# State-space stage of a decoder trunk: six output pieces in another order, column units between the inputs, a lag of 12 instead of 16, three early gated weights

## What is computed

```
u = h @ in_w                                     # 256 x 2048, in 128 groups of 16
bu = einsum('gnp,blgp->lbgn', b_bar, ug)         # inputs of the states, 64 states a group
s_t = lam_bar * s_{t-1} + bu_t                   # recurrence over the tokens
y = real(einsum('gpn,lbgn->blgp', cmat, states)) + d_skip * u
g = gelu(y)
val, gate = split(g @ glu_w + glu_b, 2)          # the gated product
mixer = val * sigmoid(gate)
mod = silu(c) @ ada_w + ada_b                    # shift, scale and gate vectors, beside all this
```

## Time and profile before

| | |
|---|---|
| three runs | median 2579.45 us (2578.98 to 2582.96) |
| the profiled execution, its own time | 2583.09 us |
| its span, first to last instruction | 2581.3 us |
| the stage from the first `inputs` to the gated product without a stop | 212.0 to 391.3 us of the span |
| TensorE's work in that stage | inputs 212 to 230, column units 230 to 302, pieces and units 302 to 374, gated product from 375.7 |
| VectorE's recurrence | 220.9 to 355.8 |

### The profile page before, as it was taken

How to read it: one execution, slowest core, us unless ns; L and a number is a source line. 1 busy time by engine, 2 the same in 40 slices (tenths; PEclk the granted TensorE clock), 3 DMA queues, 4 the chain that set the end, 5 groups by cost and what they waited for, 6 DMA issues and landing times.

```text
span 2581.3 us, 33012 instructions
## 1 busy us (share of the span) xinstructions
PE 2442.6 (95%) x12615; PEld 1949.0 (76%) x12615; DVE 1811.8 (70%) x2796; ACT 1042.2 (40%) x1217; POOL 35.2 (1%) x67
## 2 busy tenths in 40 slices
PE   5897789999999999999999999869999999999998
PEld 2474357778888888888877888748888888888886
DVE  6556968877777776877678876797777754555457
ACT  1352014464343444334453444354644344443442
POOL 0000000000000000000000000000000000000000
PEclk9998689999999999999999999779999999999999
DMA  9855978877888887888558888406598766656664
GB/s 340 324 188 213 370 279 297 280 222 258 288 286 305 277 284 270 278 283 289 191 158 287 286 279 275 149 17 209 172 312 289 257 192 191 188 190 193 191 216 147
DMA packets 310172, 627.35 MB, mean 243 GB/s; under 512 B 30240, under 2 KB 30656, under 8 KB 309760
## 3 DMA queue, kind: packets, MB, share of 16 engines
q1 hardware_dynamic: 305728, 611.35, 70.2%
q0 software_dynamic: 4288, 13.90, 1.8%
HBM read 623.05 MB, written 2.10 MB: 242 GB/s over the span
## 4 chain that ended last, share of the span: by engine, by line
PE 82%; DMA 6%; DVE 6%; issue 2%; ACT 2%; SPq 1%; DVEq 0%; ACTq 0%
PE psA L1833 37%; PE psB L1833 37%; DMA col_raw<-in_ada_w 4%; PE psM L1575 1%; PE psT L1532 1%; DMA w_raw<-in_s_glu_w 1%; DMA w_raw<-in_s_in_w 1%; DVE w_lo L951 1%; PE psM L1562 1%; DMA w_raw<-in_dsa_in_w 1%; ACT w_hi L672 1%; DVE score L1372 0%; PE psT L1719 0%; PE psM L1547 0%; DVE soft L1404 0%
## 5 line engine op out<-in xcount | busy, mean ns | idle before, releaser
L951 DVE TENSOR_TENSOR w_lo<-w_raw,w_hi 128x1024 fp32r<-128x1024 f32 x748 | 912.7, 1224 | 629.4 <-ACT w_hi L672 621.5
L672 ACT ACTIVATE w_hi<-w_raw 128x1024 fp32r<-128x1024 f32 x748 | 791.4, 1060 | 1144.8 <-PE psB L1833 474.0
L1833 PE MATMUL psA<-w_hi,hT_hi 128*128 128x512 f32 (+1 forms) x1168 | 459.4, 393 | 13.5 <-DVE hT_lo L1299 5.4
L1833 PE MATMUL psB<-w_hi,hT_hi 128*128 128x512 f32 x1152 | 455.5, 395 | 1.7 <-DVE w_lo L951 1.6
L1833 PE MATMUL psA<-w_hi,hT_lo 128*128 128x512 f32 (+1 forms) x1168 | 455.4, 390 | 0.0
L1833 PE MATMUL psA<-w_lo,hT_hi 128*128 128x512 f32 (+1 forms) x1168 | 455.0, 390 | 0.0
L1833 PE MATMUL psB<-w_hi,hT_lo 128*128 128x512 f32 x1152 | 448.8, 390 | 0.0
L1833 PE MATMUL psB<-w_lo,hT_hi 128*128 128x512 f32 x1152 | 448.4, 389 | 0.0
L968 DVE SCALAR_TENSOR_TENSOR ada_acc<-ada_raw,csil,ada_acc 128x512 f32<-128x512 f32 x420 | 314.0, 748 | 15.0 <-DVE ada_acc L968 0.5
L1833 PEld LDWEIGHTS psA<-w_hi,hT_hi 128*128 128x128 f32 x1168 | 223.0, 191 | 61.8 <-issue 13.5
L1833 PEld LDWEIGHTS psA<-w_hi,hT_lo 128*128 128x128 f32 x1168 | 222.9, 191 | 45.1
(11 more groups left out here) (345 smaller groups left out, 2118.9 us busy)
## 6 DMA issues: line engine op xcount, KB each, us to landing
w_raw<-in_ffn_w_in SPq DMA_DIRECT2D x352, 512.0 KB, 4.6
ada_raw<-in_ada_w SPq DMA_DIRECT2D x448, 256.0 KB, 4.9
w_raw<-in_ffn_w_out SPq DMA_DIRECT2D x176, 512.0 KB, 4.7
col_raw<-in_ada_w SPq DMA_DIRECT2D x160, 512.0 KB, 6.6
w_raw<-in_dsa_in_w SPq DMA_DIRECT2D x112, 512.0 KB, 5.0
w_raw<-in_s_glu_w SPq DMA_DIRECT2D x64, 512.0 KB, 5.5
w_raw<-in_s_in_w SPq DMA_DIRECT2D x32, 512.0 KB, 4.2
w_raw<-in_dsa_out_w SPq DMA_DIRECT2D x32, 512.0 KB, 5.4
```

What stands on the lines that cost most here:

```text
L672: nc.scalar.activation(high(u), w_raw[:, u % RING], ACT.Copy).then_inc(w_hi_ready, 1)
L951: V.tensor_tensor(low(u), w_raw[:, u % RING], high(u).bitcast(F32), ALU.subtract).then_inc(w_lo_ready, 1)
L1833: ins = MM(PS[s][:, t, 0:r.width], a_[:, kt, tok], b_[:, kk, 0:r.width], start=kt == 0 and m == 0, stop=k == r.units - 1 and kk == UK - 1 ...
```

## The change

- `outputs` runs in six pieces, and half 0 comes first: (half, first chunk, chunks) = (0,0,64), (1,0,64), (0,64,32), (1,64,32), (0,96,32), (1,96,32). The last four have 32 moving columns where there were 64, with as many matmuls each. `y_full` counts to 6, and the pieces carry 4, 4, 0, 2, 2 and 0 pairs of units.
- The first four column units stand behind `inputs(4)`, two more behind `inputs(5)` and two behind `inputs(6)`. To keep psM free for them, `inputs(5)` to `inputs(7)` rotate through psA, psB and psT, and wait for other counts of ScalarE's copies.
- `LEAD` is 12, `skip(0)` stands behind slot 94 and waits for `y_full` 2.
- Three gated weights are loaded early (`AHEAD` = 3), and `STATE_SLOTS` no longer holds slot 2. On VectorE `skip(2)` and `g_low(2)`, `g_low(3)` stand ahead of the first weight that isn't early; ScalarE's order changes to match.

The core of the diff:

```diff
-STATE_SLOTS = (11, 10, 9, 8, 13, 12, 6, 11, 10, 9, 8, 13, 12, 6, 2, 3)
+STATE_SLOTS = (11, 10, 9, 13, 8, 12, 6, 3) * 2
...
-LEAD = 16
+LEAD = 12
+PIECES = ((0, 0, HALF), (1, 0, HALF), (0, HALF, HALF // 2), (1, HALF, HALF // 2), (0, HALF + HALF // 2, HALF // 2),
+          (1, HALF + HALF // 2, HALF // 2))
...
         def input_bank(n, g):
 
+            if n > 4:
+                q = 4 * (n - 4) + g
+                return (PS[0], PS[1], T)[q // 2 % 3][:, q % 2]
             return (T, M)[g // 2][:, g % 2] if n % 2 else PS[g // 2][:, g % 2]
 
         def inputs_read(n):
 
-            return (2 * n, 2 * n) if n <= 4 else (8 + 4 * (n - 4), 8)
+            return (2 * n, 2 * n) if n < 4 else (10 + 4 * (n - 4), 8)
...
-                            for n in range(2):
+                            for n in range(AHEAD):
                                 sp.wait_ge(col_used, glu_after(n))
                                 w_unit(glu, 0, n)
...
-                gelu(1)
                 for n in range(2):
                     hi_unit(glu.unit + n)
-                act.wait_ge(y_full, 4)
+                act.wait_ge(col_used, glu_after(13))
+                hi_unit(glu.unit + 2)
+                act.wait_ge(col_used, 5 * VUNITS)
+                nc.scalar.activation(late_row[:, 1], M[:, 0], ACT.Copy).then_inc(rows_read, 1)
+                gelu(1)
+                act.wait_ge(y_full, len(PIECES))
                 for k in range(4):
                     g_high(k)
-                act.wait_ge(col_used, glu_after(13))
-                hi_unit(glu.unit + 2)
+                hi_unit(glu.unit + 3)
                 gelu(2)
...
-                vec.wait_ge(y_full, (1, 3, 4)[n])
+                vec.wait_ge(y_full, (2, 5, 6)[n])
...
-                    if slot == 108:
+                    if slot == 94:
                         skip(0)
                 skip(1)
-                for n in range(2):
+                for n in range(AHEAD):
                     vec.wait_ge(col_used, glu_after(11 - n))
                     lo_unit(glu.unit + n)
                 g_low(0)
                 g_low(1)
-                vec.wait_ge(col_used, glu_after(9))
-                lo_unit(glu.unit + 2)
                 skip(2)
-                for k in range(2, 8):
+                g_low(2)
+                g_low(3)
+                vec.wait_ge(col_used, glu_after(8))
+                lo_unit(glu.unit + 3)
+                for k in range(4, 8):
                     g_low(k)
...
-                col_units(FRONT, FRONT + 56)
-                outputs(0, FRONT + 56)
-                outputs(1, FRONT + 64)
+                    if n == 4:
+                        col_units(FRONT, FRONT + 4)
+                    if n in (5, 6):
+                        col_units(FRONT + 2 * n - 6, FRONT + 2 * n - 4)
+                col_units(FRONT + 8, FRONT + 56)
+                pe.wait_ge(bu_read_act, 24)
+                outputs(0, FRONT + 56, 4)
+                col_units(FRONT + 64, FRONT + 66)
+                outputs(1, FRONT + 66, 4)
+                col_units(FRONT + 74, FRONT + 80)
                 pe.wait_ge(y_read, 1)
                 pe.wait_ge(gate_ready, 1)
...
-                col_units(FRONT + 72, FRONT + 76)
-                outputs(2, FRONT + 76)
+                col_units(FRONT + 80, FRONT + 84)
+                outputs(2, FRONT + 84, 0)
                 col_units(FRONT + 84, FRONT + 88)
                 pe.wait_ge(gate_done, 4)
-                outputs(3, FRONT + 88)
+                outputs(3, FRONT + 88, 2)
+                outputs(4, FRONT + 92, 2)
+                outputs(5, FRONT + 96, 0)
```

More of the change, by code:

```diff
@@ L559, in _ @@
                         u = r.unit + i * r.per + n
-                        if r is glu and i == 0 and n < 2:
+                        if r is glu and i == 0 and n < AHEAD:
                             continue
@@ L573, in _ @@
                             if first and n == RING:
-                                sp.wait_ge(y_full, 4)
+                                sp.wait_ge(y_full, len(PIECES))
                             if i == 1 and n == 0 and r.before == "ln":
@@ L632, in _ @@
                                        ).then_inc(gbias_landed, 16)
-                    pool.wait_ge(y_full, 4)
+                    pool.wait_ge(y_full, len(PIECES))
                 if r is attn_out:
@@ L1566, in col_units @@
                     if v == 2 and k == 0:
-                        pe.wait_ge(bu_read_act, inputs_read(8)[0])
+                        pe.wait_ge(bu_read_dve, 8)
                     if v == 4 and k == 0:
@@ L1699, in inputs, with outputs @@
                 ins.then_inc(bu_full, 1)
-            def outputs(n, between):
-                half, c0 = ((1, 0), (0, 0), (0, HALF), (1, HALF))[n]
+            def outputs(n, between, pairs):
+                half, c0, width = PIECES[n]
+                fresh = n in (0, 1, 3)
+                last = n in (1, 4, 5)
                 def place(f, d):
                     if half:
-                        return T[:, f // 4 % 2, (f % 4 * 2 + d) * HALF:(f % 4 * 2 + d + 1) * HALF]
-                    return PS[f // 4][:, f // 2 % 2, (f % 2 * 2 + d) * CHUNKS + c0:(f % 2 * 2 + d) * CHUNKS + c0 + HALF]
+                        at0 = (f % 4 * 2 + d) * HALF + c0 % HALF
+                        return T[:, f // 4 % 2, at0:at0 + width]
+                    at0 = (f % 2 * 2 + d) * CHUNKS + c0
+                    return PS[f // 4][:, f // 2 % 2, at0:at0 + width]
                 per = 4 if half else 2
                 for f in range(8 * half, 8 * half + 8):
-                    MM(place(f, 1), K0[:, f], uT[:, f, 2 * c0 + 1:2 * (c0 + HALF):2], start=n != 2 and f % per == 0, stop=False)
-                pe.wait_ge(rec, rec_after(half, c0 + HALF - 1))
+                    MM(place(f, 1), K0[:, f], uT[:, f, 2 * c0 + 1:2 * (c0 + width):2], start=fresh and f % per == 0, stop=False)
+                pe.wait_ge(rec, rec_after(half, c0 + width - 1))
                 for f in range(8 * half, 8 * half + 8):
@@ L1718, in outputs @@
                                 rows = slice(32 * g, 32 * g + 32)
-                                ins = MM(place(f, d)[rows], Ctab[d][ri][:, f, rows], st[:, c0:c0 + HALF, half, g, ri, f % 8],
-                                         start=False, stop=n != 1 and f % per == per - 1 and d + ri == 2)
-                    if f % 2:
+                                ins = MM(place(f, d)[rows], Ctab[d][ri][:, f, rows], st[:, c0:c0 + width, half, g, ri, f % 8],
+                                         start=False, stop=last and f % per == per - 1 and d + ri == 2)
+                    if f % 2 and f % 8 // 2 < pairs:
                         col_units(between, between + 2)
```

2 lines of the change are left out of this document (removed).

## The result

| | before | changed |
|---|---|---|
| median of 11 runs | 2582.42 us (2578.83 to 2584.73) | 2586.73 us (2584.89 to 2590.78) |
| ratio, 95% interval | | 1.0021 (1.0012 to 1.0030) |
| profiled execution, own time | 2583.09 us | 2584.89 us |

What follows compares the result with a forecast made beforehand. TensorE bounds the stage behind the DMA-bound unit stream: +18.1 (pieces), +2.1 (waits, half clock), -8.7 (earlier stream), -6.3 (tail) give +5.1 us. Carried from 2579.45 us: 2584.6 us, range 2570.5 to 2590.

Steps and rivals of the forecast that it cites:

- the stream 8.7 us earlier: Column units between the inputs: the DMA-bound stream starts 8.7 us earlier, its last pair ending at 293.4 instead of 302.14.
- Piece 1's end at 321.1: Output pieces 0 and 1 with their unit pairs, behind the stream: piece 1 ends at 321.1, with no wait for states.
- The wait of 8.6 us before `skip(0)`: VectorE, done with slot 94 at 312.5, waits for piece 1 until 321.1; TensorE's extra pieces hide it.
- The sum at unit 3: Start of unit 3 in the gated product: 396.4 against 391.25, +5.1 us in all.
- What a piece of 32 columns costs: Narrow output pieces on TensorE: 9.0 us each, the upper bound, at 28 ns a record; lower bound 5.5 us.
- rival 1: Output pieces: pace goes with the columns, groups of pieces 2 to 5 cost 3.55 us; -8.5 us, 2571.0; chance 0.20.
- the term of +18.1 us for the split: Four output pieces become six: two more at 9.0 us of TensorE, in full on the path.
- Waits at units 72 to 79: Behind piece 1, ahead of the gate matmuls: 12.6 us for 3.5 us of work, 9.1 us of waits, until 333.7.
- The half clock: Behind the gate matmuls: two pairs and K0 of piece 2 at PEclk 0.50, 7.4 us instead of 3.7.
- The tail: Gated product: the 4.65 us stop goes; from E to unit 3 11.0 us instead of 17.35, a gain of 6.3.
- E: Start of the last output records, 1.86 us before the gated product starts: forecast 385.4 against 373.9.
- Rival 4: VectorE becomes the bound through the stall at slot 94, despite 12 us in hand; chance 0.03.

Runs made afterwards that it cites:

- kernel 9: Changed kernel, still six pieces, with skip(0) behind slot 103 instead of 94; +5.7 us against the kernel before, ratio 1.0016 to 1.0035.
- kernel 1: Changed kernel with four pieces of 64 columns instead of six; -0.8 us against the kernel before, ratio 0.9990 to 1.0008.
- kernels 1 and 5: kernel 1, and the kernel before with only the early column units and their bank rotation; the latter -0.6 us, ratio 0.9991 to 1.0008.
- kernel 7: Changed kernel with four pieces, skip(0) behind slot 103 and gelu(1) ahead of the hi_unit; -5.1 us against the kernel before, ratio 0.9975 to 0.9993.
- kernel 11: Changed kernel with the pairs of units 84 to 87 inside piece 2, not behind it; +8.3 us against the kernel before, ratio 1.0021 to 1.0046.
- kernels 2 and 11: kernel 11, and the changed kernel with gate matmuls ahead of units 72 to 79; the latter +6.2 us against the kernel before, 1.0015 to 1.0033.

## Why the forecast was right, and which of its steps were not

Steps that held, measured from the same copy of ScalarE: the stream 8.7 us earlier (8.8; but it bought only 1.3 us alone). Piece 1's end at 321.1 (318.6 + 2.5 = 321.1). The wait of 8.6 us before `skip(0)` (8.11), and that it costs nothing with six pieces (kernel 9). The sum at unit 3: +5.1, measured +5.03. That agreement is luck: errors of +5.0, +1.6 and +1.5 us stand against -5.9 and -2.3.

- **What a piece of 32 columns costs: this step failed.** I kept 28 ns a record, reading a pace that was alike at both clocks as a price of each instruction. It is the strided read, by columns; narrow pieces have 14.4 ns. The groups of pieces 2 to 5 were to take 28.5 us and take 22.6 (6.45, 5.7, 3.8, 6.6), not the 14.2 of rival 1: some 6.4 us of what the pace gives back goes into gaps of instruction supply. With four K0 of 1.9 us, the term of +18.1 us for the split is some +12. That lies between my bounds and not at either; the supply is a resource that the trace of before shows only as a queue's line.
- **Waits at units 72 to 79, under-sized by 5.0 us**: used up at 338.8 (336.22 + 2.53, in the prediction's times), not 333.7. The first pair starts at 326.4, where I had 324.4, since it came 6.8 us after the issue (317.08 to 323.84), not 5.1; for each further pair I took 2.64 us, and the intervals are 3.4, 2.7 and 4.4; and the last pair ran at half clock (1.87 us, not 1.3).
- **The half clock was put in the wrong place.** It was 0.50 from 322 to 338 of the changed kernel's span, so the gate matmuls cost 5.95 instead of 4.65, and it was over where I expected it: two pairs and K0 took 3.8 us, not 7.4. Net 2.3 us less than the sum. At the product's start it came back (0.57).
- **The tail gives less: 4.8 us instead of 6.3** (12.55 us from E to unit 3, against 17.35): units 0 to 2 took 9.9 us, not 8.2, with PEclk at 0.57 from 383 to 387. Alone it gave 3.4.
- E is at 383.7, not 385.4: 5.0 more at the units, 1.3 at the gate, 3.7 less for pairs and K0, 5.9 less for the groups, and 1.6 for pairs that ran slower, is -1.7.

Rival 1's time was wrong though its pace was right. Rival 4 took hold with four pieces only: there VectorE was the bound by 7 us. Of the loss, the split is the cause shown: kernel 1 and the changed one differ in it alone, by 5 to 6 us. That the rest of the change gains nothing with four pieces (-0.8 us) is the other half of it: the early stream's 8.8 us go into waits for units, for `skip(0)` and for the recurrence (kernels 1 and 5).

## What to carry to other kernels

A pace that ignores the clock is not yet a price for each instruction: look at the operand's stride, and change it in an experiment that keeps the rest. When work is cut into smaller instructions, count the instructions: 128 records of these matmuls come in one packet, and in the gaps of these traces TensorE went on no sooner than 3.45 us after the last one, 27 ns a record, however short they are. A stream that starts earlier pays only if the waits behind it (here a skip behind a fixed slot, the recurrence, the next loads) are moved with it; kernel 7 shows the same parts paying 0.16% once they were, in four pieces. And a lead at the head of the next phase is not yet a lead at its end: follow it through that phase's first waits and its clock.

## What I had not expected of the hardware

- TensorE reads 64 strided fp32 columns in 27.7 ns a record and 64 neighbouring ones in 14.2; at half clock 28.1 and 26.6.
- Records on 128x32 tiles follow one another in 9.7 ns with 32 neighbouring columns, and in 14.4 ns with 32 strided ones.
- TensorE runs dry of instructions for 0.4 to 3.5 us at a time beside dense small matmuls, each time ended 2 to 3 us behind a 16 KB packet of the instruction queue in the gaps read for this, of the changed kernel and kernel 11. The two longest intervals, 6.19 us in kernels 2 and 11, stand beside full DMA engines (shares 1.02 and 1.03), but so does one of the shortest; no run here changes the loads alone, so their part is not shown.
